# Mixer blocks of 384, 512, 512, 512 and 256 columns, and token rows that carry both gates and the first expert

## The reference

```python
for l in range(DEPTH):                                  # DEPTH = 2
    m = hybrid_mixer(x, ...)
    x = layer_norm(ALPHA * x + m, ln1_g[l], ln1_b[l])
    f = grouped_moe(x, router_w, router_b, exp_w_gate[l], exp_w_up[l], exp_w_down[l])
    x = layer_norm(ALPHA * x + f, ln2_g[l], ln2_b[l])
```

```python
_, idx = lax.top_k(masked, TOP_K)                               # (T,2)
gates = jax.nn.softmax(jnp.take_along_axis(logits, idx, axis=-1), axis=-1)
h = jax.nn.silu(xt @ w_gate[e]) * (xt @ w_up[e])                # 16 experts, 1024 -> 512
y = y + dense_gates[:, e:e + 1] * (h @ w_down[e])
```

## Time and profile before

| | us |
|---|---|
| median of 3 runs | 2028.21 (2025.96 to 2029.23) |
| the profiled execution, its own time | 2037.57 |
| its span, core 2, the slowest | 2036.5 |
| spans of the eight cores | 2007.5 to 2036.5 |

### The profile page before, as it was taken

The page is one execution under the profiler, slowest core; times in us unless marked ns, Lnnn a source line. Parts: engine busy times, 40 slices in busy tenths (PEclk is TensorE's granted clock), DMA queues, the critical chain, the costliest instruction groups (busy, mean ns, idle before and its releaser), DMA issues.

```text
span 2036.5 us, 23801 instructions; the slowest of 8 cores (2007.5 to 2036.5 us)
## 1 busy us (share of the span) xinstructions
PE 1260.2 (62%) x7040; PEld 640.8 (31%) x7040; DVE 1041.5 (51%) x2328; ACT 637.1 (31%) x1109; POOL 496.1 (24%) x361
## 2 busy tenths in 40 slices
PE   0577868586429698685254687767535967878200
PEld 0433333232215454342121233333223534544000
DVE  1357486757733232232279658675761322323597
ACT  0344544435202222120254254443421211211122
POOL 4011315041340000001845112303031000000597
PEclk9897879798659899897567798978766989989655
DMA  9947667759848999997965878974124999997663
GB/s 199 260 137 99 99 94 125 104 89 180 160 123 208 260 224 249 246 236 222 206 134 64 112 93 115 125 89 90 63 84 144 236 244 230 247 256 168 225 210 131
DMA packets 78766, 334.99 MB, mean 164 GB/s; under 512 B 10776, under 2 KB 22688, under 8 KB 62880
## 3 DMA queue, kind: packets, MB, share of 16 engines
q0 software_dynamic: 26384, 166.16, 50.1%
q1 hardware_dynamic: 52240, 167.14, 25.3%
HBM read 362.71 MB, written 147.19 MB: 250 GB/s over the span
## 4 chain that ended last, share of the span: by engine, by line
PE 38%; DMA 17%; DVE 16%; issue 15%; ACT 8%; POOL 3%; DVEq 0%; SPq 0%; ACTq 0%; another core or an unknown queue 0%; POOLq 0%
PE pb L596 36%; DMA yg<-s_scr 6%; DMA s_wbuf<-ew 3%; DMA s_xy<-xg 3%; DMA s_xtok<-x 2%; ACT s_scr L605 2%; PE pT L1287 1%; ACT s_xy L641 1%; DVE s_sm L624 1%; ACT L605 1%; ACT s_xtok L605 1%; DVE s_scr L609 1%; DVE s_sm L675 1%; DVE s_scr L616 1%; DVE s_xtok L609 1%
## 5 line engine op out<-in xcount | busy, mean ns | idle before, releaser
L596 PE MATMUL pb<-s_xy,s_wbuf 128*128 128x352 bf16 (+2 forms) x2992 | 657.4, 349 | 145.2 <-ACT s_scr L605 34.5
L596 PEld LDWEIGHTS pb<-s_xy,s_wbuf 128*128 128x128 bf16 x2992 | 288.6, 104 | 396.3 <-issue 237.0
L596 PE MATMUL pb<-s_wbuf,s_scrb 128*128 128x512 bf16 (+1 forms) x768 | 232.1, 399 | 51.6 <-DMA s_wbuf<-ew 28.4
L616 DVE TENSOR_SCALAR s_scr<-pb,s_gsl 128x512 f32<-128x512 f32 (+1 forms) x192 | 135.6, 745 | 234.8 <-PE pb L596 167.6
L596 PE MATMUL pb<-s_wbuf,s_xy 128*128 128x512 bf16 x792 | 239.2, 412 | 8.9 <-DVE s_xtok L624 2.2
L609 POOL TENSOR_TENSOR s_xtok<-s_xtok,s_lnp 128x1024 f32<-128x1024 f32 x76 | 183.8, 2422 | 199.8 <-ACT s_xtok L605 153.4
L609 DVE TENSOR_TENSOR s_scrb<-s_scr,pb 128x352 bf16<-128x352 f32 x128 | 64.6, 519 | 229.9 <-PE pb L596 218.8
L406 POOL DMA_DIRECT2D s_wbuf<-exp_w x42 | 22.4, 532 | 645.8 <-PE pb L596 577.8
L641 ACT COPY s_xy<-pT 128x1024 bf16<-128x1024 bf16 (+1 forms) x96 | 90.3, 940 | 283.4 <-PE pT L1287 253.2
L1287 PE MATMUL pT<-s_identb,s_xy 128*128 128x128 bf16 (+1 forms) x768 | 121.9, 226 | 89.0 <-DMA s_xy<-xg 53.2
L709 PE MATMUL pT<-s_identb,s_scr 128*128 128x128 bf16 x336 | 55.0, 273 | 182.2 <-ACT s_scr L605 70.5
(11 more groups left out here) (119 smaller groups left out, 1619.2 us busy)
## 6 DMA issues: line engine op xcount, KB each, us to landing
ew<-exp_w POOLq DMA_DIRECT2D x36, 1536.0 KB, 17.8
s_wbuf<-ew SPq DMA_DIRECT2D x54, 1024.0 KB, 14.6
s_wbuf<-exp_w POOLq DMA_DIRECT2D x42, 1024.0 KB, 15.4
yg<-s_scr SPq DMA_DIRECT2D x64, 512.0 KB, 15.0
s_xy<-xg SPq DMA_DIRECT2D x32, 514.0 KB, 13.4
yg<-s_scr SPq DMA_DIRECT2D x32, 384.0 KB, 17.8
xg<-s_gov SPq DMA_DIRECT2D x2, 5808.0 KB, 31.4
s_xtok<-x SPq DMA_DIRECT2D x17, 512.0 KB, 10.6
```

The costliest lines, as they stand in the source:

```text
L596: em.op(PE, lambda e: e.matmul(out.ap, lhsT.ap, rhs.ap, start=start, stop=stop), w=[out], r=[lhsT, rhs])
L616: em.op(E, lambda e: e.tensor_scalar(out=out.ap, in0=a.ap, scalar1=a1, scalar2=None, op0=op0), w=[out], r=rr)
```

## The change

**Blocks.** `MBLOCKS` becomes (0, 384), three of 512 and (1920, 256): the halo is the first tile of block 0. There are five blocks as before. A new `tiles_of(b)` gives the tiles of a block and leaves out tile 0 in layer 1, for G, O0, A and R. The path `state_only` goes: in layer 1 too, `CPS_section(0)` is computed in full, over 384 columns. Layer 1 now runs five of each section instead of four and the halo's short one. The correction of the first 16 means moves to block 0, behind the halo; the mask of the halo's choices is applied to tile 0 alone. The first block now reads 3 tiles of x, the second 4.

**Rows.** Instead of the k-th gate, the row carries three numbers that do not depend on k: 0.5 - 0.5 t, t (the tanh of half the difference of the two logits) and 16 numbers summed to the base slot of the first expert. The receiver compares the third with its own base: if equal, the gate is the sum of the first two, otherwise the first. The DVE copy between the two sets of scatters is gone, and with it its wait. `R_section` has three small instructions more, and `x_turn` two small DVE instructions instead of one copy. `x_load` reads 516 float32 numbers a row instead of 514.

```diff
-MBLOCKS = [(0, 128)] + [(128 + i * NB, NB) for i in range(TM // NB)]
+MBLOCKS = [(0, 384), (384, NB), (896, NB), (1408, NB), (1920, 256)]
...
+            def tiles_of(b):
+                t0, nb = MBLOCKS[b]
+                return list(range(1 if last and b == 0 else t0 // 128, (t0 + nb) // 128))
...
-                if state_only:
-                    for j in range(2):
-                        cpy(ACT, hbs[j](0, 30), hbs[j](nb, nb + 30))
-                else:
-                    pcs = [zbank(), zbank()]
-                    for k in range(31):
...
+                pcs = [zbank(), zbank()]
+                for k in range(31):
...
+                ts(DVE, gcol(0), c1(lb), -0.5, ALU.mult, 0.5, ALU.add)
+                cpy(DVE, gcol(1), c1(lb))
+                tt(DVE, v16(tmp), v16(eq1), e16(ebase()), ALU.mult)
+                rsum(la, tmp)
+                cpy(DVE, gcol(2), c1(la))
...
                 for k in range(2):
-                    xr, xf = xrow[b == nblk - 1], xrowf[b == nblk - 1]
-                    gcol = xf(0, nt * GW // 2).v(lambda ap: ap.rearrange("p (t c) -> p t c", t=nt)[:, :, D // 2:D // 2 + 1])
-                    gcol.box = xr[0](D, GW).box[:3] + (xr[nt - 1](D, GW).box[3],)
-                    cpy(DVE, gcol, ge.v(lambda ap: ap[:, k * nt:(k + 1) * nt].rearrange("p (t o) -> p t o", o=1)))
                     for t in range(nt):
...
             enter(0)
-            if skip0:
-                CPS_section(0)
-            fb = 1 if skip0 else 0
-            if fb:
-                enter(1)
-            G_section(fb)
-            CPS_section(fb)
-            O0_section(fb)
+            G_section(0)
+            CPS_section(0)
+            O0_section(0)
...
-                cpy(DVE, gsl(s * CT + j, s * CT + j + 1, 0, nj), gv.v(lambda ap: ap[0:nj, :]))
+                gv = [xgG[s](j * 516 + 512 + q, j * 516 + 513 + q).v(lambda ap: ap[0:nj, :]) for q in range(3)]
+                gs_ = gsl(s * CT + j, s * CT + j + 1, 0, nj)
+                stt(DVE, gs_, gv[2], float(e * CAP), gv[1], ALU.is_equal, ALU.mult)
+                tt(DVE, gs_, gs_, gv[0], ALU.add)
```

More of the change, by code:

```diff
@@ L880, in build @@
             last = (l == n_layers - 1)
+            def tiles_of(b):
+                t0, nb = MBLOCKS[b]
+                return list(range(1 if last and b == 0 else t0 // 128, (t0 + nb) // 128))
             def G_section(b):
                 t0, nb = MBLOCKS[b]
-                tiles = list(range(t0 // 128, (t0 + nb) // 128))
-                state_only = last and b == 0 and stop is None
+                tiles = tiles_of(b)
                 GS = 272
@@ L1167, in R_section @@
                 tt(DVE, v16(eq2), v16(msk), b16(m1), ALU.is_equal)
-                if b == 0:
-                    ts(DVE, eq1, eq1, vmask(), ALU.mult)
-                    ts(DVE, eq2, eq2, vmask(), ALU.mult)
+                if i0 == 0:
+                    for eq_ in (eq1, eq2):
+                        h16 = eq_.v(lambda ap: ap[:, 0:NE])
+                        ts(DVE, h16, h16, vmask(), ALU.mult)
                 mk, ac, cum = mka(0, n), (lambda a, c: mka(64 + a, 64 + c)), mka(128, 144)
@@ L1225, in R_section @@
                     ts(DVE, flag(l, l + 1), m1.v(lambda ap: ap[:, 0:1]), float(CAP), ALU.is_gt)
-            skip0 = last and stop is None
             def C_section(b):
@@ L1349, in build @@
                 for b, (t0, nb) in enumerate(MBLOCKS):
-                    if last and b == 0:
-                        continue
-                    tl = list(range(t0 // 128, (t0 + nb) // 128))
+                    tl = tiles_of(b)
                     pipeline(tl, xT_stages(alpha_after=True))
```

76 lines of the change are left out of this document (32 added, 44 removed).

## The result

| | before | after |
|---|---|---|
| median, us | 2027.39 of 4 runs (2025.96 to 2029.23) | 1979.46 of 4 runs (1973.26 to 1981.36) |
| the profiled execution, its own time | 2037.57 | 1980.59 |
| its span, slowest core | 2036.5 (core 2) | 1979.5 (core 3) |
| mean of the eight cores' spans | 2020.4 | 1962.9 |

The ratio is 0.9758, with a 95% interval of 0.9734 to 0.9782: the change makes the kernel 48 us, 2.4%, faster. The prediction was 33 us. The profiled executions stand 57 us apart, since that of before lay 10 us over its median and that of after 1 us.

The account below looks back on a forecast made before the run. Mixers bound by chains between DVE, ACT and PE, experts by DMA. Layer 0 -38, layer 1 +3, experts +2: -33 us from 2028.2, so 1995 us; range 1966 to 2030.

Parts of the forecast that it names:

- Layer 0, start: Start to block 0's convolution: block 1's x lands 0 to 6 us after 56.8; convolution at 64 us, before 69.25.
- Layer 0, steady part: First to last convolution of layer 0, 14 tiles: 387 us by pace, 406 by the fixed law, weighed two to one.
- the pace law: Mixer steady parts: a tile costs 27.6 or 28.5 us in whatever block; rival pace alone 1974 us, chance 0.17.
- The fixed law: Mixer steady parts: a block's period is a constant plus a part by width, 84.6 us for 384; rival 2021, chance 0.17.
- Layer 0, end: Last convolution to row load in layer 0: 56.6 us less, 95.3 instead of 151.9.
- The output matmuls, norm and turning over: End of each mixer, two tiles instead of four: 0 to 21.5 us less, taken as 15.
- The last `wm` copy ahead of the row loads: End of layer 0: the weight copy now goes out right ahead of the row loads, costing 3 us (0 to 10).
- `gsl` and the `s_dgm` products: Layer 0's experts' stage: POOL's products, some 14 us, hold DVE's `gsl` instructions; 0 to 4 us worse, left at 0.
- Layer 1, start: First gather to first convolution of layer 1: three tiles suffice instead of five, convolution at 1043, 17 us earlier.
- Layer 1, steady part: First to last convolution of layer 1, with halo computed in full: 399 us by pace, 419 by the fixed law.
- Layer 1, end: Last convolution to row load in layer 1: 98.3 us instead of 142.4, with 8.0 instead of 15.3 for the scatters.
- Experts: Experts' stages: two small DVE instructions per piece instead of one copy, 0 to 3 us a layer, taken as 1 each.

Follow-up runs that it names:

- the second group: Changed kernel again (ratio 0.975), beside it with a small copy back in inner blocks (0.9968), in last block (0.9763), or layer 0's weight copies planned at 5/6 size (0.9792).
- the kernel with closer copies: Changed kernel with the planner's size of a weight copy at 5/6: ratio 0.9813 in both layers, 0.9792 in layer 0 alone.

## Why the prediction was right, and where it was not

The direction and the range were right (1966 to 2030); the size was 15 us short. That it came so near is in part luck: of the stages, two came out 9 and 17 us dearer than predicted and the others 2 to 11 us cheaper, and the steady parts agree with the forecast only because one error cancels another. By its own steps, with the means over the cores:

- **Layer 0, start** (64 us): wrong, 71.9. The step that failed is the landing of block 1's x, "0 to 6 us more" than 56.8. The last of its tiles was issued at 32.54 and took 34.66 us, until 67.2: SP had spent the time from 8 to 24 us on four small loads that were issued one by one, 2.6 to 6.2 us each. The stage is 9 us dearer than predicted. From the chain of waits on core 3 (start us, us, what):

```profile
12.30 6.18 SPq L406
...
32.54 34.66 DMA s_xtok<-x
```

- **Layer 0, steady part**: 382.6, for 387 by the pace law and 406 by the fixed. The weight of two to one went to the wrong law. The fixed law is right for the blocks (401.9 with the old rows), and what is missing is a term of the sum: the wait between the scatters of the inner blocks, 19.3 us, which the prediction had put at nothing. It priced the wait only in the last block, where DVE stood idle before the copy; in the inner blocks of layer 0 DVE did not, and the price was paid by the rows' buffer.
- **Layer 0, end**: 95.3 predicted, 112.1 measured. The scatters: 8.0 predicted, 18.0 measured; the prediction looked at which scatters stood ahead on POOL and not at the `wm` copy issued at 536, which was ahead of them in the DMA queue. The rest of the block, 46.1 predicted, took 59.3 on core 3; with the norm's products kept off POOL the stretch to the slot numbers was 13 us shorter. The output matmuls, norm and turning over, 15 of 0 to 21.5 us, were nearer still to the upper end: from the first output matmul to the slot numbers it was 36.8 us on core 3, for 59.7 before, so 22.9 less, of which 3.4 were reckoned for the router's stall.
- **The last `wm` copy ahead of the row loads**: 3 us predicted (0 to 10), 7.2 measured. The mechanism was right. The stage from the row load to the first gather holds it in full: in the second group, on one chip, it is 363.2 us in the changed kernel and 356.2 to 356.3 in the three kernels whose first turn comes after 5.1 to 5.3 us. That it is still 3.2 us shorter than before has another cause, which was not found.
- **`gsl` and the `s_dgm` products**: left at 0, and it was 0. The products were over at 574.9, the rows came at 585.1. A DVE product of 128x512 with two inputs in SBUF, ahead of them, lasted 14.63 us beside POOL's 13.87, where it had taken 0.68 us before (at 564.51). By the Trainium skill, "SBUF — State Buffer", section "Who interferes with whom", a DVE instruction with two inputs in SBUF contends with a GpSimd instruction that reads SBUF, and these rows agree.
- **Layer 1, start**: 17 us predicted, 27.7 measured. From the third tile's copy (994.93 on core 3) to the convolution (1011.62) it was 16.7 us, for 18.8 reckoned. What was missed is that the third tile itself comes earlier, probably since the halo's own pass no longer stands among the first tiles: 54.5 us after the first gather (940.44), 62.8 before.
- **Layer 1, steady part**: 401.9, for 399 and 419. The same two errors as in layer 0: 419.2 with the old rows, and 17.3 us for the wait.
- **Layer 1, end**: 98.3 predicted, 86.1 measured. The scatters were right (7.7 for 8.0). To the first output matmul it was 50.4 for 52.6 on core 3, and from there to the slot numbers 28.7 instead of the 37.7 reckoned: here two tiles fewer are worth 24 us, not 15.
- **Experts**: 1 us a layer predicted. What the two `gsl` instructions cost can't be seen. The stretch from the row load of layer 1 to the end lay between 472 and 486 us in all the kernels here, and between 472 and 475 for the changed one alone, while a change elsewhere moved it by up to 8; so the 7.4 us gained in it are not put down to the change.

Of the signs named beforehand, the last convolution of layer 0 (451 to 470), the missing copy and the scatters of layer 1 came as said; the first convolution, the 8 us of layer 0 and its block of 256 did not. Two signs of being wrong came: block 1's x landed at 67.2, and in layer 1 the period behind the block of 384 is 103 us. The latter was a poor test, for the fixed law itself gave 100 there (122.1 - 22.0). In layer 0 that period is 80.7 us; the 100.7 us into the block of 256 belong to the full block ahead of it.

## What to carry to other kernels

A wait that a planner has scheduled around doesn't show as idle time: ask what buffer stays occupied over it, in every block, and not only how long an engine stands. When a stage is shortened, look for what runs beside it at its own pace, here 22 weight copies, since the new end may lie where they end; and look for when that train could have left, by the stretches in which the DMA engines are idle. Two laws that differ by 20 us can both fit a result, if another term is missing; a run with one part alone is cheap against that.

## What the runs showed of the hardware

- Scatters that POOL issued behind a copy of 1.5 MB were noticed 14 us after their issue, where without one it is 3 us (558.80 to 572.95, 1498.54 to 1501.53). A row load that SP issued beside such a copy took 11.6 to 18 us instead of 4.7.
- A DVE instruction with one tensor and one column as its inputs (128x256, float32) lasted 2.43 us beside a product of POOL and 0.41 us without. The Trainium skill, "SBUF — State Buffer", section "Who interferes with whom", lets `tensor_scalar` contend with GpSimd only where it runs in a two-port mode, and then it blocks fully; the row agrees with such a block, and no run here shows the mode.
- Copies of 1.5 MB with a change from float32 to bf16, two at a time, followed one another every 14.7 us (441.04 behind 425.70 and 411.61 in the kernel with closer copies), with the DMA engines busy 0.98 of the time at 115 GB/s (170 to 460 us, core 3).
